# Tokens held in four phases instead of two around a depthwise convolution, on eight cores

## The chip, the cores and the metric

The kernel runs on all 8 cores of one Trainium2 chip. Each core computes half of one of the four sequences (2048 of 4096 tokens), with no exchange between cores. The metric is the device time in microseconds of the slowest core. Before the change the median of three runs is 989.3 us (989.25 to 990.63).

## The reference, cut to what matters

```python
h = concat([meta_tokens(16), x], axis=1)               # per sequence, T = 16 + 4096, 1024 channels
u = rms_norm(h, g_mix)
z = u @ w_in                                           # 1024 -> 5 * 1024
a = z[..., :1024] * sigmoid(z[..., 1024:2048])         # GLU
a = depthwise_conv(a, w_dw, width 31, centred) + b_dw  # 1024 channels
a = silu(layer_norm(a, ln_g, ln_b))                    # statistic over the 1024 channels of a token
y_conv = a @ w_conv_out
p = z[..., 2048:3072]
m = window_mean(p, 2 / 4 / 8 / 16 per 256 channels) - p
y_pool = (einsum(m, w_pool) * pool_scale) @ w_pool_out
gA, gB = sigmoid(z[..., 3072:] + b_gate)
h = h + (gA * y_conv + gB * y_pool) @ w_o
v = rms_norm(h, g_ffn)
h = h + (silu(v @ w_ffn_gate) * (v @ w_ffn_up)) @ w_ffn_down     # d_ff = 2816
out = rms_norm(h, g_final)[:, 16:]
```

## The kernel before, in words

Channels lie on the 128 partitions (8 chunks `c` of 128 channels), tokens along the free dimension. A core takes its 2048 tokens plus a halo, `EXT` = 2080 columns. The tokens are kept in two phases: `uT` is `[128, 8, 2, 1040]`, all even tokens of a chunk and then all odd ones.

A small recorder (`Sched`) takes every operation in the order in which the Python emits it, adds the semaphore waits that its reads and writes need, and replays the list of each engine. So each engine works strictly in emission order; `op` and `dma` (lines 164 and 172) are the helpers, and all records carry the line of a helper: L370 is every matmul but the convolution's (L664), L381 every ScalarE activation, L384, L391 and L397 VectorE or GpSimd operations, L199 a DMA issue. Eight PSUM banks exist: banks 6 and 7 hold statistics, and `nb()` hands out the other six in a ring, so a matmul tile waits until the tile six before it has been read out. Work that is not urgent (the pooling windows, the layer norm steps) sits in a list `bg`, and `pump(n)` emits the next n of its items on the spot.

The order is: the start (`START`, a list written out by hand: squares, RMS statistic, normalised `uT`, and the `pool` projections); then for each chunk `c` the stage of the convolution (lines 682 to 693): `vg(c)` computes value and gate in five pieces of 416 tokens into `aT`, GpSimd writes `aT` to a DRAM scratch `ad` in two DMAs (`a_out`), `conv(c-2)` runs, and then SyncE issues `im2col(c)`: 16 DMAs that read `ad` back into `rep`, each channel four times, shifted by one column each. `rep` has four buffers (two for each chunk; the last chunk has two of its own), so `im2col(c)` fills what `conv(c-2)` has just read.

The convolution (`conv`, line 653) is a matmul against a sparse weight: one rhs row is one of 16 channels, 2 phases and 4 shifts (16 x 8 = 128 rows), so one matmul covers 8 taps, and four of them (`q`) cover 31. The output has 32 columns (16 channels by 2 phases), and four such matmuls (`j`) fill the 128 PSUM partitions next to each other. A group `g` of 64 channels has two tiles of 512 columns, read out by two ScalarE operations each (`d` and its square `dsq`), and VectorE adds them up in `acc_s` and `acc_q`.

After the last `conv(7)`: four tiles of gate B, the layer norm statistic (`ln_stat`: a matmul with `pmask` sums over partitions of the same phase, for two halves of 512 columns), `fold(g)` (folds `w_pool` into `w_pool_out`, into `weff`), gate tiles, and among them the steps of `ln_steps` (subtract the mean on VectorE or GpSimd, multiply with 1/std, then `silu` on ScalarE and a DMA by SyncE which brings rows of 64 channels by 2 phases into rows of 128 channels, `cell`). `P` is the pool product with `weff`, `C` the convolution's output product, which needs the `cell` DMAs. The output projection and the feed-forward part follow.

The source of one read-back DMA and its destination are (lines 648 to 651):

```python
for j in range(4):
    for r in range(2):
        src = bass.AP(a_d, (128 * c + 64 * i + 16 * j) * EXT + HE * r, [[EXT, 16], [1, 4], [1, RW]])
        S.dma(SP, rep_sem[r_i], rep[r_i][r::2, j, 0:RW], src, val=tot)
```

Of the kernel before, what the change touches and what calls it, by code (L numbers as in the profile page):

```python
# [22 lines left out]
HALO = 15  # L23
# [3 lines left out]
HE = EXT // 2  # L27
HP = PW // 2
# [13 lines left out]
RW = TOK // 2 + 12  # L42
RWP = 1040
# [8 lines left out]
PC_BDW, PC_LNG, PC_LNB = 48, 64, 80  # L52
PC_COLS = 96
# [148 lines left out]
def build_nc():  # L202
# [18 lines left out]
    cw_d = din("cw", [NG, 128, 512])  # L221
# [3 lines left out]
    a_d = nc.dram_tensor("ad", [KC, 128, 2, HE], BF16, kind="Internal")  # L225
# [34 lines left out]
    oW = reserve(16384)  # L260
# [4 lines left out]
    uT = at("uT", [128, KC, 2, HE], BF16, oA)  # L265
# [3 lines left out]
    mT = at("mT", [128, KC, 2, TOK // 2], BF16, oM)  # L269
# [4 lines left out]
    def dof(g, h):  # L274
        return oB + (g // 2) * EXT * 4 + (2 * (g % 2) + h) * 2048

    d_sb = [at(f"d{g}", [128, 2 * TT], F32, dof(g, 0)) for g in range(NG)]
    cell = [at(f"cell{c}", [128, 2, 2, 2, TT], BF16, oB + c * EXT * 4) for c in range(KC)]
    actX = [[cell[g // 2][:, g % 2, h, 0, :] for h in range(2)] for g in range(NG)]
    actT = [[cell[c][:, b % 2, b // 2, 1, :] for b in range(NB)] for c in range(KC)]  # L280
    mrg = [[cell[c][:, b % 2, b // 2, 0, :] for b in range(NB)] for c in range(KC)]
    acc_s = at("acc_s", [128, TOK // 2], F32, oW)
    acc_q = at("acc_q", [128, TOK // 2], F32, oW + 4096)
    pmask = at("pmask_s", [128, 128], F32, oW + 8192)
    cw = [at(f"cw{i}", [128, 4, 4, 32], BF16, oW + 8704 + i * 1024) for i in range(3)]
    cw.append(alloc("cw3", [128, 4, 4, 32], BF16))
# [8 lines left out]
    rep = [at(f"rep{i}", [128, 4, RWP], BF16, o) for i, o in  # L295
           enumerate((z, z + 8 * RWP, oB + 6 * EXT * 4, oB + 7 * EXT * 4, z + 24064, z + 32384))]
    z += 2 * 4 * RWP * 2
    dsq = [at("dsq0", [128, 2 * TT], F32, z), at("dsq1", [128, 2 * TT], F32, oW + 11776)]
# [3 lines left out]
    aT = [at(f"aT{i}", [128, 2, HE], BF16, z + i * EXT * 2) for i in range(2)]  # L302
# [3 lines left out]
    z += 2 * S_W * 4  # L306
    assert z <= oZ + NZT * 2048, (z - oZ, NZT * 2048)
# [225 lines left out]
    def s1_norm(p, h):  # L533
        o, n = PIECES[p]
        for k in range(4 * h, 4 * h + 4):
            stt(DVE, uT[:, k, :, o // 2:(o + n) // 2], par(xb[p][:, k, :]), pcc(PC_GMIX, k), par(psum[7][:, 0:n]),
                ALU.mult, ALU.mult)

    def pool_tile(p, c):
        o, n = PIECES[p]  # L540
        b = nb()
        for k in range(KC):
            mm(par(b[:, 0:n]), w(f"pool{c}", k), uT[:, k, :, o // 2:(o + n) // 2], k == 0, k == KC - 1)
# [6 lines left out]
    def windows(c, ti):  # L550
# [8 lines left out]
        m = mT[:, c, :, t0 // 2:(t0 + n) // 2]  # L559
# [52 lines left out]
    def load_cw(g):  # L612
        S.dma(POOL, cw_sem[g % 4], cw[g % 4][:].rearrange("p j q m -> p (j q m)"), cw_d.ap()[g])
# [25 lines left out]
    def im2col(c):  # L639
# [5 lines left out]
        for i in range(2):  # L645
            r_i = rix(2 * c + i)
            tot = rep_sem[r_i].count + 16 * 8
            for j in range(4):
                for r in range(2):
                    src = bass.AP(a_d, (128 * c + 64 * i + 16 * j) * EXT + HE * r, [[EXT, 16], [1, 4], [1, RW]])  # L650
                    S.dma(SP, rep_sem[r_i], rep[r_i][r::2, j, 0:RW], src, val=tot)

    def conv(c):
        pump_until(win_done, c)
        for g in (2 * c, 2 * c + 1):
            for h in range(2):
# [17 lines left out]
            elif g > 1:  # L674
                tt(DVE, acc_s[:], acc_s[:], d_sb[g][:], ALU.add)
# [478 lines left out]
```

How the kernel before makes its waits and increments, by code:

```python
def replay(e, rec):  # L190
    for o in rec.ops:
        if o[0] == "wait":
            e.wait_ge(o[1], o[2])
        elif o[0] == "ins":
            r = o[1](e)
            if o[2]:
                r.then_inc(rec.sem, 1)
        else:
            e.dma_start(out=o[1], in_=o[2]).then_inc(o[3], 16)
```

## Time and profile before

| | before |
|---|---|
| median of 3 runs | 989.3 us (989.25 to 990.63) |
| the profiled execution, its own time | 991.0 us |
| span of its slowest core (core 0) | 989.5 us |
| spans of all cores | 985.5 to 989.5 us |
| TensorE busy / VectorE / ScalarE / GpSimd | 97% / 44% / 29% / 16% |
| TensorE clock granted, core 0 | 0.997 on average |
| DMA moved | 105.81 MB |

The span runs from the first to the last instruction of a core. A matmul of 512 columns is recorded with 379 ns, but these overlap: what counts is the distance from one to the next. The rows that the prediction uses stand in a section of their own below.

### The profile page before, as it was taken

The page shows a single profiled execution, that of the slowest core. Times are in us where ns is not written, and L with a number is a line of the kernel's source. Part 1 is how long each engine was busy: PE and PEld are TensorE (multiplying, and loading weights), DVE is VectorE, ACT ScalarE, POOL GpSimd, SP SyncE. Part 2 cuts the span into 40 slices and gives each one's busy share as a digit, 9 for nine tenths or more (in the row PEclk, how much of TensorE's full clock was granted, in tenths as well). Part 3 has the DMA queues.
Part 4 walks back from the last instruction along what each step waited for, and adds up shares of the span by engine and source line. Part 5 has one row for each costly group of instructions (what it writes and reads, how often), then busy time and mean ns, then how long its engine had stood idle before and what let it go on. Part 6 is the DMA issues. An engine that isn't in the chain of part 4 may idle for free.

```text
span 989.5 us, 14699 instructions; the slowest of 8 cores (985.5 to 989.5 us)
## 1 busy us (share of the span) xinstructions
PE 962.3 (97%) x5176; PEld 474.0 (48%) x5176; DVE 433.1 (44%) x632; ACT 291.7 (29%) x486; POOL 154.9 (16%) x216
## 2 busy tenths in 40 slices
PE   3999999999899999999999999999999999999996
PEld 2755555554344444444444444444444444444485
DVE  4776689653885323233476212211112211342454
ACT  3853143356952121110544111111111111121121
POOL 3002221124740000001771110110000000000000
PEclk9999999999999999999999999999999999999999
DMA  9705988775773111226965444553222005122222
GB/s 212 233 4 98 217 215 177 231 171 119 132 170 62 22 20 24 32 32 155 356 165 133 74 82 90 101 98 47 34 31 43 12 1 181 75 85 85 85 86 85
DMA packets 41158, 105.81 MB, mean 107 GB/s; under 512 B 5760, under 2 KB 14208, under 8 KB 38400
## 3 DMA queue, kind: packets, MB, share of 16 engines
q0 software_dynamic: 21472, 51.06, 28.7%
q1 hardware_dynamic: 19616, 53.82, 16.3%
q8 instruction: 43, 0.70, 0.3%
q14 instruction: 27, 0.22, 0.1%
HBM read 115.80 MB, written 21.04 MB: 138 GB/s over the span
## 4 chain that ended last, share of the span: by engine, by line
PE 95%; DMA 2%; DVE 1%; POOL 1%; issue 1%; ACT 0%; DVEq 0%; ACTq 0%; POOLq 0%
PE ps L370 92%; PE ps L664 3%; DMA xb<-xp 1%; DMA wslot<-w_pool_out 1%; DVE uT L397 0%; POOL d L384 0%; DVE h2b L397 0%; POOL wslot L199 0%; ACT sqx L381 0%; DVE sqx L384 0%; ACT ps L381 0%; ACT sq L381 0%; DVE h2b L384 0%; DVEq L1033 0%; DVEq L193 0%
## 5 line engine op out<-in xcount | busy, mean ns | idle before, releaser
L370 PE MATMUL ps<-vT,wslot 128*128 128x512 bf16 x1408 | 304.4, 379 | 0.0
L370 PE MATMUL ps<-uT,wslot 128*128 128x416 bf16 (+3 forms) x1536 | 292.3, 349 | 3.1 <-DVE uT L397 2.3
L370 PEld LDWEIGHTS ps<-uT,wslot 128*128 128x128 bf16 x1536 | 151.1, 99 | 140.8 <-issue 12.6
L370 PEld LDWEIGHTS ps<-vT,wslot 128*128 128x128 bf16 x1408 | 137.7, 98 | 167.1 <-issue 1.6
L384 DVE TENSOR_TENSOR fT<-ps,sgf 128x512 bf16<-128x512 f32 x88 | 60.7, 691 | 228.8 <-PE ps L370 228.8
L370 PE MATMUL ps<-fT,wfd 128*128 128x512 bf16 (+1 forms) x880 | 153.2, 336 | 0.0
L381 ACT ACTIVATE sgf<-ps 128x512 f32<-128x512 f32 x88 | 52.5, 597 | 241.5 <-PE ps L370 234.2
L370 PEld LDWEIGHTS ps<-fT,wfd 128*128 128x128 bf16 x880 | 86.1, 98 | 67.8 <-issue 1.7
L370 PE MATMUL ps<-cell,wslot 128*128 128x512 bf16 x512 | 114.8, 379 | 0.0
L397 DVE SCALAR_TENSOR_TENSOR zt<-zt,ps 128x512 f32<-128x512 f32 x64 | 43.9, 687 | 106.1 <-PE ps L370 106.0
L381 ACT ACTIVATE zt<-ps,hb 128x512 f32<-128x512 f32 x64 | 43.9, 691 | 138.1 <-PE ps L370 138.1
L370 PEld LDWEIGHTS ps<-cell,wslot 128*128 128x128 bf16 x512 | 50.1, 98 | 61.1 <-issue 1.1
L370 PE MATMUL ps<-mT,weff 128*128 128x512 bf16 x256 | 59.8, 381 | 0.0
L381 ACT ACTIVATE sq<-h2b 128x512 f32<-128x512 f32 (+1 forms) x35 | 19.1, 544 | 105.4 <-DVE h2b L384 105.4
L384 DVE TENSOR_TENSOR h2b<-ps,h2b 128x512 f32<-128x512 f32 (+1 forms) x40 | 23.2, 583 | 61.4 <-PE ps L370 51.2
L199 POOL DMA_DIRECT2D wslot<-w_in x40 | 22.7, 584 | 150.7 <-PE ps L370 149.8
L199 POOL DMA_DIRECT2D wslot<-w_ffn_up x22 | 11.8, 537 | 202.1 <-PE ps L370 202.1
L381 ACT ACTIVATE sg<-ps 128x416 f32<-128x416 f32 x40 | 20.9, 524 | 75.1 <-PE ps L370 63.0
L370 PEld LDWEIGHTS ps<-mT,weff 128*128 128x128 bf16 x256 | 25.3, 99 | 30.9 <-issue 1.1
L384 POOL TENSOR_TENSOR ac<-ac,sq 128x512 f32<-128x512 f32 x28 | 35.7, 1274 | 20.1 <-ACT sq L381 18.3
L384 DVE TENSOR_TENSOR aT<-ps,sg 128x416 bf16<-128x416 f32 x40 | 23.6, 589 | 33.8 <-PE ps L370 30.2
L384 DVE TENSOR_TENSOR ac<-ac,sq 128x512 f32<-128x512 f32 (+1 forms) x34 | 20.1, 590 | 28.3 <-ACT sq L381 28.3
(76 smaller groups left out, 610.6 us busy)
## 6 DMA issues: line engine op xcount, KB each, us to landing
rep<-ad SPq DMA_DIRECT2D x128, 129.5 KB, 4.7
wslot<-w_in POOLq DMA_DIRECT2D x40, 256.0 KB, 7.0
h1d<-h1b SPq DMA_DIRECT2D x4, 2048.0 KB, 10.1
h2b<-h1d SPq DMA_DIRECT2D x4, 2048.0 KB, 13.7
h1b<-xr SPq DMA_DIRECT2D x3, 2048.0 KB, 19.6
out<-h2b SPq DMA_DIRECT2D x3, 2048.0 KB, 8.1
wslot<-w_ffn_gate POOLq DMA_DIRECT2D x22, 256.0 KB, 5.3
wslot<-w_ffn_up POOLq DMA_DIRECT2D x22, 256.0 KB, 5.2
```

Of the source, the lines that this page charges most:

```text
L199: e.dma_start(out=o[1], in_=o[2]).then_inc(o[3], 16)
L370: S.op(PE, lambda e: e.matmul(out, lhsT=lhsT, rhs=rhs, start=start, stop=stop), [lhsT, rhs], [out], signal=stop if signal is None else signal)
L381: S.op(ACT, lambda e: e.activation(out=out, in_=in_, func=func, scale=scale, **kw), reads, [out])
L384: S.op(eng, lambda e: e.tensor_tensor(out=out, in0=a, in1=b, op=op), [a, b], [out])
L397: S.op(eng, lambda e: e.scalar_tensor_tensor(out=out, in0=a, scalar=s, in1=b, op0=op0, op1=op1), [a, b] + ([] if isinstance(s, float) else ...
L664: S.op(PE, lambda e, o=o, lt=lt, r_=r_, q=q, j=j: e.matmul(o, lhsT=lt, rhs=r_, start=(q == 0), stop=(q == 3), tile_position=(0, 32 * j)), ...
```

## The change

The number of phases goes from 2 to 4 (`PH`), in all layouts that hold tokens in the mixer part (`uT`, `aT`, `ad`, `mT`, `cell`, the host's `xp`, `xr` and `out`). A 16-column shift replaces the 15-column one (`HALO`). A convolution row is now 8 channels by 4 phases by 4 shifts, that is 16 token positions; 31 taps need three matmuls per tile instead of four. A tile is 32 channels (`i`) by 4 phases, with all 512 columns. The layer norm statistic covers 512 columns at once, after VectorE has added the two tiles (`i`) of `acc_s` and of `acc_q`. `silu` works on four blocks of 256 columns per chunk and half, each followed by its own DMA. Reads and writes of `psb` (float32, tokens in order) go through `alt` with a step of 4 elements instead of 2.

```diff
-HALO = 15
+HALO = 16
+PH = 4
...
-HE = EXT // 2
-HP = PW // 2
+HE = EXT // PH
+HP = PW // PH
...
-RW = TOK // 2 + 12
+RW = TT + 5
...
-    a_d = nc.dram_tensor("ad", [KC, 128, 2, HE], BF16, kind="Internal")
+    a_d = nc.dram_tensor("ad", [KC, 128, PH, HE], BF16, kind="Internal")
...
-    uT = at("uT", [128, KC, 2, HE], BF16, oA)
+    uT = at("uT", [128, KC, PH, HE], BF16, oA)
...
     def par(ap):
-        return ap.rearrange("p (e x) -> p e x", e=2)
+        return ap.rearrange("p (e x) -> p e x", e=PH)
 
     def alt(ap):
-        return ap.rearrange("p (x e) -> p e x", e=2)
+        return ap.rearrange("p (x e) -> p e x", e=PH)
+
+    def two(ap):
+        return ap.rearrange("p (f x) -> p f x", f=2)
...
-            for j in range(4):
-                for r in range(2):
-                    src = bass.AP(a_d, (128 * c + 64 * i + 16 * j) * EXT + HE * r, [[EXT, 16], [1, 4], [1, RW]])
-                    S.dma(SP, rep_sem[r_i], rep[r_i][r::2, j, 0:RW], src, val=tot)
+            for j in range(8):
+                src = bass.AP(a_d, (128 * c + 64 * i + 8 * j) * EXT, [[1, 4], [HE, 32], [1, RW]])
+                S.dma(SP, rep_sem[r_i], rep[r_i][:, j, 0:RW], src, val=tot)
...
-            for h in range(2):
+            for i in range(2):
                 ps = nb()
-                for q in range(4):
+                for q, x0 in enumerate((0, 4, 5)):
                     for j in range(4):
                         o = ps[32 * j:32 * j + 32, :]
-                        lt = cw[g % 4][:, j, q, :]
-                        x0 = h * TT + 4 * q
-                        r_ = rep[rix(g)][:, j, x0:x0 + TT]
+                        lt = cw[g % 4][:, i, q, j, :]
+                        r_ = rep[rix(g)][:, 4 * i + j, x0:x0 + TT]
...
-    def ln_stat(h):
-        tok = slice(h * TT, (h + 1) * TT)
-        pm, pq = (nb(), nb()) if h else (psum[6], psum[7])
-        mm(pm[:], pmask[:], acc_s[:, tok], True, True)
-        mm(pq[:], pmask[:], acc_q[:, tok], True, True)
...
+    def ln_stat():
+        pm, pq = psum[6], psum[7]
+        for acc, ps in ((acc_s, pm), (acc_q, pq)):
+            tt(DVE, acc[:, :, 0, :], acc[:, :, 0, :], acc[:, :, 1, :], ALU.add)
+            mm(two(ps[:]), pmask[:], acc[:, :, 0, :], True, True)
...
     def silu(h, c):
-        for g in (2 * c, 2 * c + 1):
-            act(actX[g][h], dpart(g, h), AF.Silu, bias=pc[:, PC_LNB + g:PC_LNB + g + 1],
-                scale=pc[:, PC_LNG + g:PC_LNG + g + 1])
-        for g in (2 * c, 2 * c + 1):
-            r0 = 64 * (g % 2)
-            S.dma(SP, rg_sem[h * KC + c], cell[c][r0:r0 + 64, :, h, 1, :], actX[g][h], val=32)
+        for q in range(4):
+            G = 4 * c + q
+            act(cell[c][:, h, q, 0, :], dcell[c][:, h, q, :], AF.Silu, bias=pcc(PC_LNB, G), scale=pcc(PC_LNG, G))
+        for q in range(4):
+            S.dma(SP, rg_sem[h * KC + c], cell[c][32 * q:32 * q + 32, h, :, 1, :], cell[c][:, h, q, 0, :], val=64)
...
-            if g == 0:
-                if h:
-                    cp(DVE, psum[6][:], mean)
-                    cp(DVE, psum[7][:], rstd)
-                    zfree.append(ids[1])
...
     for g in range(4):
         wps_scale(g)
     Bm(0, 0)
     Bm(0, 1)
     Bm(0, 2)
-    for h in range(2):
-        ln_stat(h)
+    ln_stat()
     Bm(0, 3)
     release("gB0")
-    for h in range(2):
-        ln_rstd(h)
+    ln_rstd()
     bg.extend(ln_steps(0))
     bg.extend(ln_steps(1))
```

## Rows read from the trace of the kernel before

**Rows 1.** The page: TensorE in all, and in 40 slices of the span.

```profile
PE 962.3 (97%) x5176; PEld 474.0 (48%) x5176; DVE 433.1 (44%) x632; ACT 291.7 (29%) x486; POOL 154.9 (16%) x216
PE   3999999999899999999999999999999999999996
```

**Rows 2.** TensorE's waits: what for, us in total, times, longest.

```profile
PE ps L370 <- DMA wslot<-w_pool_out: 2.5, 1, 2.5
```

**Rows 3.** Timeline of TensorE, 125 to 250 us: start, duration, form, count.

```profile
128.55 14.24 PE L370 MATMUL ps<-uT,wslot 128*128 128x416 bf16 x80
...
146.30 14.51 PE L370 MATMUL ps<-uT,wslot 128*128 128x416 bf16 x80
...
235.02 3.64 PE L664 MATMUL ps<-rep,cw 128*32 128x512 bf16 x64
238.59 5.37 PE L370 MATMUL ps<-uT,wslot 128*128 128x512 bf16 x24
243.80 1.02 PE L370 MATMUL ps<-acc_s,pmask_s 128*128 128x512 f32 x2
...
247.23 1.89 PE L370 MATMUL ps<-uT,wslot 128*128 128x512 bf16 x8
```

**Rows 4.** The read-back's DMA issues on SyncE: ns, first and last start.

```profile
L199 SPq DMA_DIRECT2D rep<-ad x128: 514/594/1903, 101.2 to 229.7; - x128
```

**Rows 5.** The same DMAs, 214 to 240 us: issue to landing, minimum, median, maximum.

```profile
DMA to landing us min/median/max: 3.9/5.6/6.7
```

**Rows 6.** DMA queues from 101 to 235 us: packets, MB, share of 16 engines.

```profile
q1 hardware_dynamic: 10240, 16.98, 42.5%
q0 software_dynamic: 5616, 10.28, 40.7%
```

**Rows 7.** DMA rate from 143 to 161 us, in 40 slices.

```profile
GB/s 169 114 246 92 134 194 252 120 4 9 36 105 100 168 105 114 159 159 153 123 157 233 211 154 106 113 308 382 364 382 355 336 318 318 327 318 308 290 249 32
```

**Rows 8.** Timeline of VectorE: in brackets its idle time before, and who ended it.

```profile
145.83 1.23 DVE L384 TENSOR_TENSOR acc_s<-acc_s,d 128x1024 f32<-128x1024 f32 x1 [1.14 <-ACT d L381]
...
155.70 0.58 DVE L384 TENSOR_TENSOR aT<-ps,sg 128x416 bf16<-128x416 f32 x1
...
173.51 0.59 DVE L384 TENSOR_TENSOR aT<-ps,sg 128x416 bf16<-128x416 f32 x1
...
238.25 1.33 DVE L384 TENSOR_TENSOR acc_s<-acc_s,d 128x1024 f32<-128x1024 f32 x1 [11.72 <-ACT d L381]
```

**Rows 9.** Groups by form: count, busy us, mean ns; idle before, releaser.

```profile
L381 ACT ACTIVATE cell<-d,pc_s 128x512 bf16<-128x512 f32 x32 | 24.3, 814 | 6.0 <-DVE d L384 6.0
L381 ACT ACTIVATE sq<-h2b 128x512 f32<-128x512 f32 x21 | 13.2, 630 | 78.3 <-DVE h2b L384 78.3
L381 ACT ACTIVATE sq<-h2b 128x256 f32<-128x256 f32 x14 | 5.8, 417 | 27.1 <-DVE h2b L384 27.1
L397 DVE SCALAR_TENSOR_TENSOR mT<-s,psb 128x1024 bf16<-128x1024 f32 x12 | 14.7, 1223 | 0.4
L384 DVE TENSOR_TENSOR s<-s 128x1024 f32<-128x1024 f32 x12 | 14.6, 1220 | 0.5
```

**Rows 10.** Timeline of ScalarE, GpSimd and TensorE around the folds.

```profile
252.57 0.71 ACT L381 ACTIVATE acc_q<-acc_q,eps_s 128x512 f32<-128x512 f32 x1
...
267.54 1.09 ACT L381 ACTIVATE weff<-ps 128x512 bf16<-128x512 f32 x2
...
252.98 6.20 POOL L384 TENSOR_TENSOR d<-d,zt 128x512 f32<-128x512 f32 x5
259.13 0.59 POOL L199 DMA_DIRECT2D wslot<-w_pool_out  x1
...
265.50 2.93 PE L370 MATMUL ps<-wslot,wslot 128*128 128x512 bf16 x7 [2.49 <-DMA wslot<-w_pool_out]
268.22 14.45 PE L370 MATMUL ps<-mT,weff 128*128 128x512 bf16 x64
```

**Rows 11.** One stretch: busy us of PE, PEld, DVE, ACT, POOL; clock; DMA share; GB/s.

```profile
259.00:268.00 9.00, 6.33 (x25) 2.58 (x24) 8.69 (x15) 9.00 (x15) 7.67 (x11) 0.88 0.81 153
```

More of the change, by code:

```diff
@@ L259, in build_nc @@
     oM = reserve(KC * TOK * 2)
-    oW = reserve(16384)
+    oW = reserve(16896)
     oS = reserve(NSLOT * 2048)
@@ L294, in build_nc @@
     z = oZ
[L295 to L298, printed above, removed]
+    RB = 16 * HE
+    rep = [at(f"rep{i}", [128, 8, HE], BF16, o) for i, o in
+           enumerate((z, z + RB, oB + 6 * EXT * 4, oB + 7 * EXT * 4, z + 24064, z + 32384))]
+    z += 2 * RB
+    dsq = [at("dsq0", [128, 2, 2, 256], F32, z), at("dsq1", [128, 2, 2, 256], F32, oW + 8192)]
     z += 4096
@@ L301, in build_nc @@
     z += 2 * PW * 4
-    aT = [at(f"aT{i}", [128, 2, HE], BF16, z + i * EXT * 2) for i in range(2)]
+    aT = [at(f"aT{i}", [128, PH, HE], BF16, z + i * EXT * 2) for i in range(2)]
     z += 2 * EXT * 2
@@ L733, in C @@
         stt(DVE, zt[i][:], zt[i][:], 1.0, ps[:], ALU.add, ALU.mult)
-        tt(DVE, mrg[c][b], zt[i][:], zt[j][:], ALU.add)
+        tt(DVE, mrg[c][b], two(zt[i][:]), two(zt[j][:]), ALU.add)
         zfree.append(i)
@@ L786, in send @@
         def send(n):
+            mean = half2(zt[ln_ids[1]], h)
             while sent[0] < min(n, len(far)):
@@ L944, in build_nc @@
             for k in range(KC):
-                mm(ps[:], w(f"wo{c}", k), mrg[k][b], k == 0, k == KC - 1)
+                mm(two(ps[:]), w(f"wo{c}", k), mrg[k][b], k == 0, k == KC - 1)
             h = h1b[b][:, c, :]
@@ L1078, in _host_inputs @@
     for col, v in ((PC_BDW, arr("b_dw")), (PC_LNG, arr("ln_g")), (PC_LNB, arr("ln_b"))):
-        pc[:, col:col + NG] = np.repeat(v.reshape(NG, 64), 2, 1).T
-    zero = np.zeros((1, D), f32)
-    wdw = arr("w_dw")
-    taps = np.stack([np.concatenate([wdw, zero], 0), np.concatenate([zero, wdw], 0)], 0)
-    vals = taps.reshape(2, 4, 8, NG, 4, 16).transpose(3, 5, 2, 4, 1, 0)
-    cw = np.zeros((NG, 16, 8, 4, 4, 16, 2), f32)
-    for i in range(16):
-        cw[:, i, :, :, :, i, :] = vals[:, i]
+        pc[:, col:col + 2 * NG] = np.repeat(v.reshape(2 * NG, 32), PH, 1).T
+    wdw = arr("w_dw").reshape(KW, NG, 2, 4, 8)
+    cw = np.zeros((NG, 4, 8, PH, 2, 3, 4, 8, PH), f32)
+    for q in range(3):
+        for a in range(4):
+            if q == 2 and a < 3:
+                continue
+            for pi in range(PH):
+                for po in range(PH):
+                    tap = PH * (4 * q + a if q < 2 else 8) + pi - 1 - po
+                    if 0 <= tap < KW:
+                        for ch in range(8):
+                            cw[:, a, ch, pi, :, q, :, ch, po] = wdw[tap, :, :, :, ch]
     pmask = np.zeros((128, 128), f32)
-    pmask[0::2, 0::2] = 1.0 / D
-    pmask[1::2, 1::2] = 1.0 / D
+    for e in range(PH):
+        pmask[e::PH, e::PH] = 1.0 / D
     T = SEQ + NMETA
@@ L1135, in _gather @@
 def _gather(results, core):
-    o = np.asarray(results[core]["out"]).reshape(2, 2, 128, KC, TT)
-    return o.transpose(0, 4, 1, 3, 2).reshape(TOK, D)
+    o = np.asarray(results[core]["out"]).reshape(2, 2, 128, KC, 2, 256)
+    return o.transpose(0, 5, 1, 4, 3, 2).reshape(TOK, D)
 _NC_CACHE = {}
```

116 lines of the change are left out of this document (60 added, 56 removed).

## The prediction

> **What bounds the kernel now.** I read the page first: TensorE is busy for 962.3 of 989.5 us, and outside the first slice it has almost no hole [rows 1]. So the time is TensorE's work plus what it waits for; a change is worth what it takes from TensorE's row, unless something beside TensorE is nearly late already. For the slowest core, the waits name one pause in the middle, 2.5 us for a load of `w_pool_out` [rows 2]. Then I looked at what runs beside TensorE in the stages that the change touches, and found four things near their limit.
>
> First, the read-back into `rep`. Its 128 DMAs are issued from 101.2 to 229.7 us [rows 4], and the last ones take 3.9 to 6.7 us to land [rows 5], so `rep` for group 15 is complete near 234.4. TensorE needs it halfway through conv(7), at 235.02 + 1.78 = 236.8 [rows 3]: 2.4 us of slack. From 101 to 235 the hardware queue carries 16.98 MB in 42.5% of sixteen engines, the software queue (weights, `ad`, `cw`) 40.7% [rows 6]; together 83%.
>
> Second, VectorE. It idles 1.14 us before 145.83 and not again before the next two rows, and frees the first value bank of vg(4) at 155.70 + 0.58 = 156.3 and that of vg(5) at 174.1 [rows 8]. TensorE wants the first for its fourth pair, 7 tiles of 1.42 us after 146.30, at 156.2. That is why vg(4) takes 14.51 us [rows 3], where vg(2), the same eighty matmuls, takes 14.24.
>
> Third, VectorE after conv(7): its last two pairs of additions start at 238.25 and run back to back, four of about 1.23 us, to 243.2 [rows 8], and the statistic's matmuls begin at 243.80 [rows 3]. Fourth, ScalarE and GpSimd around the folds: the slot for the late `w_pool_out` load is asked for only when GpSimd has done five subtractions, and ScalarE is busy for all 9.00 us from 259 to 268 [rows 10, 11].
>
> **The change part by part.**
>
> *Fewer convolution matmuls.* conv(7) goes from 235.02 to 238.59 [rows 3], 3.57 us for 16 groups of four matmuls side by side, 0.223 us each. Twelve groups take 2.68, so 0.89 is saved, 7.1 us over eight chunks.
>
> *One statistic.* The fp32 matmuls take 247.23 - 243.80 = 3.43 us [rows 3]; half goes, -1.7. But the sum needs another VectorE addition first (0.65 us). Today VectorE is done 8.2 us after conv(7) starts [rows 3, 8]; with tiles that come a little sooner and the addition it is about 8.6. TensorE is there after 2.68 + 5.2 = 7.9, and waits 0.7. Net -1.0. Behind it stands only gate tile Bm(0,3), which is merely shifted.
>
> *Smaller silu.* A 512-column activation of this group is busy for 24.3/32 = 0.76 us; 256 columns less save 630 - 417 = 0.21 [rows 9], so four of 0.55 replace two of 0.76: +0.7 us of ScalarE per chunk and half. Five chunks lie ahead of the last `weff` copy (+3.4), and one Ln and Exp go (-1.3, the span from 252.57 to the next copy). ScalarE reaches the copy at 267.54; P(0,0) wants its result at its seventh matmul, 268.22 + 1.3 = 269.5 [rows 10]. The copy would end near 270.1: +0.6. The bounds are 0 (the load hides it) and +2.1. Their DMAs double in number at half the size; SyncE issues one in about 0.6 us [rows 4], 19 us a half beside about 20 us of `silu`, hidden.
>
> *More blocks in a moving operand* (four for two, two for one). Cut in two, 416 columns take (14.24 - 0.07)/80 = 177 ns, 0.426 a column; uncut, 512 take (243.80 - 238.59)/24 = 217 ns, 0.424 [rows 3]. I take nothing; at 1 ns a cut the 2300 matmuls concerned would cost 2 us.
>
> *Steps of four elements.* `psb` is written and read at 16 bytes apart instead of 8. At 8 bytes it costs nothing: 1223 ns against 1220 for the form without steps [rows 9]. No row shows 16. Bounds: nothing, or double the 1.07 us in which 1024 elements stream. I take nothing, since the nearest row shows nothing; the other end is a rival. The Trainium skill (SBUF — State Buffer, Door 1: The DMA port swizzle) says lines are 16 bytes and full bandwidth wants two hits in each, and then that fp32 may step by 4 for free; by the first half this edit costs, by the second it doesn't. No row decides.
>
> *The read-back.* The count (16 a chunk) and the bytes stay (64 rows of 2072 bytes become 128 of 1034). But the order of the source changes. Before, the outermost extent of the source pattern is 16 channels and the destination has 64 partitions; now the source begins with `[1, 4]`, four shifts, against 128 partitions. If the hardware queue deals a DMA out over the engines by the outermost extent, it finds 16 shares before and 4 now, and all read-back goes through the same four of sixteen engines. Nothing in the trace has such a form, so the price is bounded: nothing if it is dealt out by rows, and otherwise this. The fastest slice with mainly read-back shows 382 GB/s [rows 7]; a quarter is 95.5 GB/s, and 16.98 MB take 178 us. The four engines also carry their share of the software queue, 40.7% of 134 us = 54.5 us in today's crowd [rows 6], perhaps half of it when twelve engines idle: I take 41. 178 + 41 = 219 us. The low end is 178 + 27 = 205; the high end takes today's shares whole: 0.425 x 134 x 4 + 54.5 = 282. I take four engines as the likelier: sixteen divides the outermost extents that this queue's read-back has today (16 and 64), so its even spread is just what dealing by the outermost extent gives, and it would give four now. The Trainium skill (DMA: Bandwidth & Descriptors, Why a DMA increments its semaphore by 16 and not by 1) states the rule: the engine count is the largest number up to 16 that divides the slowest dimension of both sides, 16 before and 4 after. No row here shows a transfer with fewer than 16 shares, so the trace neither confirms nor contradicts it.
>
> **The sum.** The stage becomes bound by the queue. im2col(c) can be issued as soon as im2col(c-1) is through, since TensorE's 16.9 us per chunk are less than 219/8 = 27. The read-back begins at 101.2, so group 15 lands at 320.2 instead of being used at 236.8: +83.4 us. The savings of conv(0) to conv(6), and all of VectorE's tightness, vanish in waits of about 10 us before each convolution. What follows counts fully: half of conv(7) -0.45, statistic -1.0, ScalarE +0.6, and after a pause TensorE starts at half clock: in 259 to 268 it waited 2.5 us and was granted 0.88 [rows 10, 11], 1.1 us lost; after 10 us of pause I take 1.7. Together +0.8. Span 989.5 + 84.2 = 1073.7; the profiled execution's 991.0 becomes 1075.2, and the median, 1.7 below it, 1073.5 us. With the stage's ends: 1059 to 1137.
>
> **The rivals.**
>
> *All engines still share the read-back: faster.* For it: every read-back today spreads well (382 GB/s [rows 7]), bytes and DMA count are the same. Against it: the extent of four. The time: conv -7.1. VectorE gives part back: its dense run starts only 1.1 us sooner (0.89, and 0.25 for the smaller tile), while TensorE comes 1.8 us sooner to vg(4) and 2.7 to vg(5), so about 1.5 us is waited [rows 3, 8]. Statistic -1.0, ScalarE +0.6. TensorE reaches group 15 by 2.2 us sooner relative to the last `ad` write, against 2.4 us of slack [rows 3 to 5]: +0.3. Sum -5.8: 983.5 us. It decides from the first conv: if `rep` lands within some 17 us per chunk, this case holds.
>
> *The step of 16 bytes costs double, with all engines: no change.* VectorE has 1.07 us more for each of eight `mT` operations before 181 us, in a stage where it has no slack: backlog +1.6 at vg(4), +3.7 at vg(5) against today, where TensorE would be 1.8 and 2.7 earlier. That eats 6.4 of 7.1 us. ScalarE's writes of `psb` grow by what they stream, 0.21 us per 256 columns [rows 9]; for those in the crowded start I put 1.5, between nothing and 5 (24 of them). -0.7 - 1.0 + 0.6 + 0.3 + 1.5 = +0.7: 990 us. For it: a step never shown; against it: 8 bytes cost 3 ns in 1220 [rows 9].
>
> **How the numbers follow.** Four engines 0.68, all engines and faster 0.20, the step 0.12. The likeliest gives 1073.5, its own range is 1045 to 1137. The range over the cases runs from 981 to 1125, since the other two hold three in ten. A measurement here tells about 0.2% from no change. Faster: 0.20 + 0.03; same: 0.05; slower: the rest, 0.72.
>
> **What would show it.** Four engines: in the rows of `rep` the time from issue to landing well over 6 us and the last issue near 310 us; TensorE waiting for a DMA into `rep` before each conv, about 10 us; the mean DMA share from 101 to 320 near a quarter plus the weights; TensorE's clock below 1.00 behind the pauses. After conv(7) a tail of about 752 us. The matmuls: 384 on `rep`, 2.68 us a chunk if not waiting. The step: `mT` operations at 1223 ns or above 2000, the writes of `psb` about the same or markedly longer. The forecast is wrong if the last `rep` DMA is issued before 240, and its size if the stage lasts less than 205 or more than 282 us.

## The result, and the profile after

The changed kernel takes 1130.0 us (median of 1120.7, 1130.0 and 1130.1) against 989.9 for the kernel before in the same session: ratio 1.1385, 95% interval 1.134 to 1.143. It is slower by 140 us. A fourth run took 1151.1 us: in some runs of every kernel one die is slower at a lower clock whatever the kernel, and all medians and ratios from here on are without those runs. I had forecast slower, 1073.5 us, with 1125 as the upper end; the median lies 5 us beyond it, and one of the three runs inside.

The slowest core (core 5) has a span of 1128.1 us. First the page: TensorE in all and by 40 slices, and the chain that ended last. They answer to [rows 1].

```profile
PE 999.3 (89%) x5044; PEld 477.2 (42%) x5044; DVE 445.5 (39%) x631; ACT 316.1 (28%) x514; POOL 155.7 (14%) x216
...
PE   4788947566718999999999999999999999999997
...
PEclk9988978888757788999999999999999999999999
...
PE 75%; SPq 13%; DMA 4%; DVE 3%; issue 2%; ACT 2%; POOL 0%; DVEq 0%; ACTq 0%; POOLq 0%
```

The row `PEclk` is the granted clock in tenths. TensorE has 132 fewer matmuls on record and is busy longer, because its clock is lower (0.928 on average for 0.997). Its holes lie in slices 1 to 12, and SyncE's queue (SPq), which only issues DMAs, is 13% of the chain. The waits of TensorE say on what (compare [rows 2]):

```profile
PE ps L677 <- DMA rep<-ad: 81.7, 9, 15.4
PE ps L376 <- DVE sqx L390: 13.6, 3, 12.7
PE ps L376 <- DVE uT L403: 12.8, 14, 3.4
PE ps L677 <- DVE acc_s L390: 6.5, 1, 6.5
...
PE ps L376 <- DMA wslot<-w_pool_out: 1.1, 1, 1.1
```

The wait for the read-back is the forecast one. The one for `uT` is not: it was 2.3 us before. The read-back's issues (to hold against [rows 4]), and the queues while it runs (against [rows 6]):

```profile
L199 SPq DMA_DIRECT2D rep<-ad x128: 511/1384/7177, 126.7 to 354.0; - x128
```

```profile
q0 software_dynamic: 5854, 11.56, 26.2%
q1 hardware_dynamic: 16896, 16.94, 21.4%
```

The first issue comes at 126.7 instead of 101.2, the last at 354.0 instead of 229.7, and the median issue takes 1384 ns for 594. In the 236 us of the second view the read-back uses 21.4% of sixteen engines; if four engines carry it, that is 0.214 x 236.3 x 4 = 202 us for each. With an even share of the software queue (0.262 x 236.3 = 62) it would be 264 us, 12% more than the stage has, so that queue's work isn't spread evenly or packet times overlap; these shares alone don't show that the four are full. The run e2 below shows it.

TensorE's timeline in that stage (compare [rows 3]): the second group of each convolution waits, and its 24 matmuls then take 2.75 us, where 24 unpaused ones take 1.49 (in 229.5 to 232.1 us the granted clock is 0.50).

```profile
212.57 1.49 PE L677 MATMUL ps<-rep,cw 128*32 128x512 bf16 x24
229.42 2.75 PE L677 MATMUL ps<-rep,cw 128*32 128x512 bf16 x24 [15.36 <-DMA rep<-ad]
232.10 14.57 PE L376 MATMUL ps<-uT,wslot 128*128 128x416 bf16 x80
...
363.49 2.75 PE L677 MATMUL ps<-rep,cw 128*32 128x512 bf16 x24 [3.00 <-DMA rep<-ad]
```

VectorE's timeline shows what I had not forecast (compare [rows 8]): it waits for TensorE before it writes `uT`, and for the scratch DMA before the fourth piece of `aT`.

```profile
84.02 4.82 DVE L403 SCALAR_TENSOR_TENSOR uT<-xb,pc_s,ps 128x448 bf16<-128x448 f32 x8 [11.47 <-PE ps L376]
...
139.77 0.59 DVE L390 TENSOR_TENSOR aT<-ps,sg 128x416 bf16<-128x416 f32 x1 [8.24 <-DMA ad<-aT]
```

Two stretches of the kernel after, and then the first of them in the kernel before (columns as in [rows 11]):

```profile
52.00:90.00 38.00, 31.13 (x140) 15.17 (x140) 18.64 (x26) 19.09 (x25) 0.00 (x0) 0.81 0.00 0
...
366.20:437.90 71.70, 69.51 (x259) 28.34 (x256) 48.05 (x74) 50.23 (x94) 34.37 (x36) 0.80 0.54 108
```

```profile
52.00:90.00 38.00, 38.00 (x205) 20.15 (x204) 28.52 (x35) 17.06 (x29) 4.25 (x8) 1.00 0.36 58
```

So the 138.6 us between the spans of the two slowest cores fall into three parts, each from start and end times of the timelines: the start, up to the first read-back, 126.7 - 101.2 = +25.5; the stage, from there to the end of conv(7), 239.5 for 137.4 = +102.1; and all after it, 761.9 for 750.9 = +11.0.

The third part isn't the change's. It stands in cores 4 and 5 alone: behind conv(7) they take 762 us each, the other six cores 750 to 751, and the cores of the kernel before 749 to 751. The stretch from above in core 3 and in core 4:

```profile
366.20:437.90 71.70, 67.98 (x302) 29.73 (x301) 50.97 (x80) 50.82 (x94) 30.85 (x34) 0.98 0.57 118
```

```profile
366.20:437.90 71.70, 69.47 (x258) 28.32 (x259) 49.38 (x77) 49.62 (x92) 32.79 (x35) 0.81 0.55 111
```

The first two parts stand in all cores: the read-back begins at 125.3 to 129.2 us (98.3 to 101.2 before), and the stage lasts 237 to 245 us (137.4 to 137.9 before).

The costs by form (compare [rows 9]). `mT` took 1223 ns before; the three `psb` forms took 584, 406 and 564.

```profile
L403 DVE SCALAR_TENSOR_TENSOR mT<-s,psb 128x1024 bf16<-128x1024 f32 x12 | 24.0, 1996 | 0.4
L390 DVE TENSOR_TENSOR aT<-ps,sg 128x416 bf16<-128x416 f32 x40 | 23.6, 589 | 65.4 <-DMA ad<-aT 38.1 <-PE ps L376 14.4 <-ACT sg L387 6.9
```

```profile
L387 ACT ACTIVATE cell<-d,pc_s 128x256 bf16<-128x256 f32 x64 | 33.1, 599 | 2.0 <-DVE d L390 2.0
...
L387 ACT ACTIVATE psb<-ps 128x448 f32<-128x448 f32 x16 | 15.7, 983 | 14.7 <-PE ps L376 14.7
L387 ACT ACTIVATE psb<-ps 128x256 f32<-128x256 f32 x24 | 15.1, 630 | 9.8 <-PE ps L376 9.3 <-DVE sqx L390 0.5
...
L387 ACT ACTIVATE psb<-ps 128x416 f32<-128x416 f32 x8 | 7.4, 920 | 9.2 <-PE ps L376 9.2
```

### The profile page after: what moved, and what is told of

It reads as the page before. It is cut to its first block, busy times and chain, and to the rows that moved or that the text cites. A ratio compares the mean times of both kernels' runs of the same rounds, so it can differ in the third digit from the quotient of the medians.

```text
span 1128.1 us, 14541 instructions; the slowest of 8 cores (1113.6 to 1128.1 us)
## 1 busy us (share of the span) xinstructions
PE 999.3 (89%) x5044; PEld 477.2 (42%) x5044; DVE 445.5 (39%) x631; ACT 316.1 (28%) x514; POOL 155.7 (14%) x216
## 4 chain that ended last, share of the span: by engine, by line
PE 75%; SPq 13%; DMA 4%; DVE 3%; issue 2%; ACT 2%; POOL 0%; DVEq 0%; ACTq 0%; POOLq 0%
PE ps L376 74%; SPq L199 13%; DMA rep<-ad 3%; DVE uT L403 1%; DMA ad<-aT 1%; ACT cell L387 1%; DMA xb<-xp 1%; DVE sqx L390 1%; PE ps L677 1%; ACT ps L387 0%; DVE mT L403 0%; ACT psb L387 0%; DVE h2b L403 0%; ACT sqx L387 0%; ACT weff L387 0%
## 5 line engine op out<-in xcount | busy, mean ns | idle before, releaser
L376 PE MATMUL ps<-uT,wslot 128*128 128x416 bf16 (+3 forms) x1536 | 316.5, 363 | 17.0 <-DVE uT L403 12.8
L376 PEld LDWEIGHTS ps<-uT,wslot 128*128 128x128 bf16 x1536 | 154.6, 101 | 178.0 <-issue 72.9
L376 PE MATMUL ps<-cell,wslot 128*128 128x512 bf16 x512 | 117.4, 385 | 0.0
L677 PE MATMUL ps<-rep,cw 128*32 128x512 bf16 x384 | 36.1, 531 | 88.2 <-DMA rep<-ad 81.7
L376 PE MATMUL ps<-mT,weff 128*128 128x512 bf16 x256 | 64.1, 400 | 1.1 <-ACT weff L387 1.0
L677 PEld LDWEIGHTS ps<-rep,cw 128*32 128x32 bf16 x384 | 12.0, 118 | 108.6 <-issue 105.3
L387 ACT ACTIVATE d<-ps,pc_s 128x512 f32<-128x512 f32 x32 | 22.1, 690 | 96.8 <-PE ps L677 96.6
L387 ACT ACTIVATE psb<-ps 128x256 f32<-128x256 f32 (+2 forms) x48 | 38.2, 796 | 33.8 <-PE ps L376 33.3
L390 DVE TENSOR_TENSOR acc_s<-acc_s,d 128x1024 f32<-128x1024 f32 x14 | 17.1, 1224 | 72.9 <-ACT d L387 72.7
## 6 DMA issues: line engine op xcount, KB each, us to landing
rep<-ad SPq DMA_DIRECT2D x128, 129.2 KB
h1d<-h1b SPq DMA_DIRECT2D x4, 2048.0 KB, 10.3
```

The source lines that it names most:

```text
L376: S.op(PE, lambda e: e.matmul(out, lhsT=lhsT, rhs=rhs, start=start, stop=stop), [lhsT, rhs], [out], signal=stop if signal is None else signal)
L387: S.op(ACT, lambda e: e.activation(out=out, in_=in_, func=func, scale=scale, **kw), reads, [out])
L390: S.op(eng, lambda e: e.tensor_tensor(out=out, in0=a, in1=b, op=op), [a, b], [out])
L677: S.op(PE, lambda e, o=o, lt=lt, r_=r_, q=q, j=j: e.matmul(o, lhsT=lt, rhs=r_, start=(q == 0), stop=(q == 2), tile_position=(0, 32 * j)), ...
```

## The experiments

Ratios are to the kernel before, run beside each (990.6 to 991.1 us). "A", "B", "L" and "S" in the expectations are the theories each names.

**The order of the source alone.** The changed kernel with channels outermost, and the kernel before with shifts outermost (weight rows permuted to match in both):

```diff
-                src = bass.AP(a_d, ..., [[1, 4], [HE, 32], [1, RW]])          # after
+                src = bass.AP(a_d, ..., [[HE, 32], [1, 4], [1, RW]])          # e1
-                    src = bass.AP(a_d, ..., [[EXT, 16], [1, 4], [1, RW]])     # before
+                    src = bass.AP(a_d, ..., [[1, 4], [EXT, 16], [1, RW]])     # e2
```

> The changed kernel with one edit: the source of the read-back begins with 32 rows instead of 4 shifts ([[HE, 32], [1, 4], [1, RW]]), and the convolution weights' rows are put in the same order. DMA count, bytes and the 1034-byte pieces stay. Theory (outermost extent of 4 confines the read-back to four engines): the time from issue to landing of a rep DMA falls back to 3 to 9 us, the waits of 82 us for rep go, the clock stays at 1.00 in the convolution stage. The start (126.7 us instead of 101.2 before the first read-back) doesn't change, since it lies ahead of it, so about 989 + 25 - 5 = 1005 to 1015 us. Rival (short or unaligned pieces are slow on any number of engines): stays above 1100 us.

> The kernel before with the one property added: the source of the read-back begins with the 4 shifts ([[1, 4], [EXT, 16], [1, RW]]), weight rows reordered to match; two phases, 2072-byte pieces, everything else as before. Theory (four engines): the stage becomes bound by the queue, 128 DMAs of 16 pieces per engine at 85 to 109 ns give 174 to 222 us plus the software queue's share of 55 to 80, against 134 us today: 1080 to 1150 us. Rival (it is the four phases, not the order): stays at 989 us.

e2 measured 1073.5 us, ratio 1.083 [1.082, 1.085]. Its waits and its issues:

```profile
PE ps L664 <- DMA rep<-ad: 65.6, 7, 13.7
```

```profile
L199 SPq DMA_DIRECT2D rep<-ad x128: 507/1214/3768, 101.1 to 305.5; - x128
```

The order alone, with two phases, costs 82.8 us, and its stage is 220.7 us from the first issue to the end of conv(7), against 137.4: +83.3. This is the forecast mechanism at the forecast size. In the last part of its stage, where little but the read-back runs, the sixteen engines are busy for about a quarter, and the rate (last column, GB/s) is about a quarter of the 382 of [rows 7]:

```profile
284.00:296.00 12.00, 3.90 (x36) 1.41 (x40) 2.36 (x2) 2.54 (x4) 0.00 (x0) 0.64 0.26 99
```

e1 measured 1052.2 us, ratio 1.061 [1.058, 1.063]. The read-back now lands in 5.1 us, its issue takes 603 ns in the median, and no wait for `rep` is left among TensorE's large ones; still the kernel is 61 us slower than before and 37 above the end of what I expected, with its first read-back at 130.4. So a second cause exists:

```profile
PE ps L677 <- DVE aT L390: 19.7, 6, 4.5
...
PE ps L376 <- DVE uT L403: 12.5, 13, 3.4
PE ps L376 <- DVE aT L390: 9.0, 3, 7.1
```

**Is the second cause the step of 16 bytes?** e3 puts such steps into the kernel before, e4 takes them out of e1. In both the pooling branch gets its tokens in another order and computes something else.

```diff
+        return ap.rearrange("p (x e f) -> p e f x", e=2, f=2)     # e3: psb written and read in steps of 4
-        return ap.rearrange("p (x e) -> p e x", e=PH)             # e1
+        return ap.rearrange("p (e x) -> p e x", e=PH)             # e4: no step
```

> The kernel before, but psb is written by ScalarE and read by VectorE for mT with a step of 4 float32 (16 bytes) instead of 2, in the same number of elements and operations. The tokens of the pooling branch end up in another order, so that branch computes something else. Theory (the 16-byte step is what makes psb 796 instead of 470 ns and mT 1996 instead of 1223 ns): those two groups show the longer durations, the first read-back is issued 15 to 25 us later than at 101.2, time 1003 to 1015 us. Rival (the late start comes from the four-block uT and PSUM patterns or something else of the change): 989 to 991 us.

> The changed kernel with the read-back order of e1 and, besides, psb written and read without a step (the rows of psb are kept in phase order as blocks, so the pooling windows add up the wrong tokens: that branch computes something else). All else of the change is in. Theory (four engines and the 16-byte step are all that costs): the sum of the fast case holds, 7.1 us of convolution, 1.0 of statistic saved, 1.5 waited for VectorE, less than 1 at the folds: 982 to 986 us, faster than before by 0.4 to 0.7%. Rival (the change has further costs, such as more blocks per operand, twice the silu DMAs, or ScalarE at the folds): 989 us or more.

e3: 994.5 us, ratio 1.0037 [1.0023, 1.0050]. e4: 1056.4 us, 1.0625 [1.0574, 1.0676], no better than e1. The step costs 3.8 us by itself and is not the second cause. In e4 VectorE stands idle 59.2 us for the DMA that reads `aT`.

**The recorder's granule.** VectorE writes one piece of `aT` while a DMA reads another; they share no byte. But the recorder tracks reads and writes in granules of `GRAN` = 32 bytes. With two phases a row of `uT` is 2080 bytes and a piece of `aT` 416 bytes, both multiples of 32. With four they are 1040 and 208, odd multiples of 16, so that neighbours share a granule, and the recorder adds a wait. With `GRAN = 16` the instructions stay as they are and only such waits go; `s_pe`, `s_act` and `s_dve` are semaphores of engines, those with `d_` of DMAs. For instance:

```text
-L403 SCALAR_TENSOR_TENSOR uT<-xb_101,pc_s,ps 128x4x64 [waits s_act,d_x1,s_pe]
+L403 SCALAR_TENSOR_TENSOR uT<-xb_101,pc_s,ps 128x4x64 [waits s_act,d_x1]
-L390 TENSOR_TENSOR aT_116<-ps,sg_115 128x4x104 [waits s_pe,s_act,s_dve,d_ad0]
+L390 TENSOR_TENSOR aT_116<-ps,sg_115 128x4x104 [waits s_pe,s_act]
```

e5 is the changed kernel with that one line, e6 has the order as well, e7 also lacks the step (pooling as in e4), and e8 gives the kernel before a granule of 64 bytes, in which its own pieces (13 x 32 bytes) share.

```diff
-GRAN = 32
+GRAN = 16        # e5, e6, e7;   GRAN = 64 in e8
```

> The changed kernel with one edit: the recorder tracks reads and writes in granules of 16 bytes instead of 32 (GRAN). In the changed layouts a phase row of uT is 1040 bytes and a piece of aT 208 bytes, odd multiples of 16, so neighbouring pieces share a 32-byte granule, and the recorder adds waits between operations that touch no common byte. Not an instruction changes, only waits. The read-back still begins with the 4 shifts. Theory B (e1 stands 62 us above before because of these waits): the first read-back is issued near 101 us, the aT operations no longer wait for the ad DMA, and the time falls from 1130 to what the four engines alone cost, as in e2: 1065 to 1085 us. Rival (the waits are harmless, e1's excess comes from other parts of the change): 1125 us or more.

> The changed kernel with both edits: granules of 16 bytes and the read-back's source beginning with the 32 rows. It computes the reference. Theory B: what is left of the costs is the 16-byte step (3.8 us in e3 at most), so 982 to 990 us, and the fast case's sum less the step would be 987. Rival (something else of the change costs): above 995 us.

> As e6, and psb without a step, as in e4 (the pooling branch computes something else). Theory: the fast case of the sum, 982 to 986 us, 2 to 5 us below e6. Rival (the step costs nothing here since VectorE has room once the convolution's rhythm is set by TensorE): within 1 us of e6.

> The kernel before with one edit: granules of 64 bytes instead of 32. Its phase row of uT is 2080 bytes and its piece of aT 416 bytes, odd multiples of 32, so the same neighbours share a granule as in the changed kernel at 32. Same instructions, only waits are added. Theory B: the same waits appear (VectorE's uT for TensorE, aT for the ad DMA), the start takes 20 to 30 us longer and the convolution stage 30 to 40: 1030 to 1060 us. Rival: within 5 us of 989.

e8: 1031.4 us, ratio 1.041 [1.040, 1.043], as expected. The kernel before, its layout untouched, gets the same waits and starts its read-back at 126.0 instead of 101.2:

```profile
PE ps L370 <- DVE uT L397: 10.8, 12, 3.4
PE ps L664 <- DVE aT L384: 10.0, 4, 4.3
PE ps L370 <- DVE aT L384: 3.2, 2, 2.2
```

e5: 1101.4 us, 1.111 [1.110, 1.113], above the 1065 to 1085 expected; e6: 1010.8 us (1012.8 over all its runs, the figure in the expectations that follow), 1.0205 [1.019, 1.022], above 982 to 990; e7: 1009.0 us, 1.018 [1.017, 1.020], above 982 to 986. Together with e1 this is a square:

| | shifts outermost | channels outermost |
|---|---|---|
| granule 32 | 1130.0 (after) | 1052.2 (e1) |
| granule 16 | 1101.4 (e5) | 1010.8 (e6) |

The order costs 78 to 91 us, the granule 29 to 41. In the 1130.0 stand some 10 us of the tail of two cores; against the run at 1120.7 the granule costs 19 and the order 69 in that row and column. The granule costs less beside the four engines, since there its part in the stage is hidden under the queue and only its start counts: e5 begins its read-back at 103.3, 23.4 us sooner than the changed kernel, while its stage lasts no less (245.4 us). In e5 TensorE's large waits in the stage are all for `rep` (99.7 us, 10 times).

**The row length on four engines.** e5 and e2 both have the shifts outermost and no added waits, yet e5 is 28 us slower, nearly all of it in the stage: 242 to 245 us by core, 216 to 221 in e2. Their read-back queues, e2 from 101.1 to 312 us, then e5 from 103.3 to 343:

```profile
q1 hardware_dynamic: 8488, 16.56, 21.1%
```

```profile
q1 hardware_dynamic: 16832, 16.88, 21.3%
```

If four engines carry them, e2 has 0.211 x 210.9 x 4 = 178 us of it on each and e5 0.213 x 239.7 x 4 = 204. A row of 2072 bytes takes 84 ns of an engine (share x 16 x window / packets), one of 1034 takes 49, 1.16 times as much per byte. That is as large as the difference of the stages. But no run changes the row length alone on four engines, and e5 also has 12% more in the software queue (11.5 for 10.3 MB).

**What is left: 1010.8 against the 983.5 of my case in which all engines share.** The queues from 101 to 245 us, first e6, then the kernel before with its rows of 2072 bytes cut in two (g1, 101 to 240 us; [rows 6] is the uncut one):

```profile
DMA  9999999999999899998899987997989998999984
...
q1 hardware_dynamic: 18432, 16.95, 50.4%
q0 software_dynamic: 5580, 11.06, 42.9%
```

```profile
DMA  8999889889999899983499962998549788499992
...
q1 hardware_dynamic: 18432, 16.98, 44.5%
q0 software_dynamic: 5616, 10.28, 39.6%
```

In e6 (core 1, its slowest) the engines are busy 93% of the stage, with hardly a gap to catch up in. The runs g1, g2, g4 and g5 add this load to the kernel before, or take it from e6.

```diff
-                for r in range(2):                                   # before
+                for x in (0, RW // 2):                               # g1: 128 rows of 1036 bytes a DMA
+                    src = bass.AP(a_d, ... + x, [[HE, 32], [1, 4], [1, RW // 2]])
...                                                                   # g2: g1, scratch writes cut in two,
+    cw_d = din("cw", [NG, 128, 768])                                 #     192 KB of weights a group
                                                                      #     (some buffers move to make room)
-            if g + 4 < NG:                                           # e6
-                load_cw(g + 4)                                       # g4: only the first four loads
+                n = 16 if j >= 4 and 2 <= c < KC - 1 else 32         # g5: a quarter fewer rows, c = 2 to 6
```

> The kernel before, in two phases, with each read-back row of 2072 bytes brought as two of 1036 by two DMAs; 16 DMAs a chunk as before, outermost extent 32, so all sixteen engines; the weight rows are reordered to match. Same bytes, twice the rows, that is the shape of the changed kernel's read-back and nothing else of it. Theory A (what is left between 1012.8 and the 984 of the fast case is the DMA stage, full because 1034-byte rows take more engine time per byte): the hardware queue's share from 101 us to the last read-back rises from 42.5% to about 52% and the sum with the software queue to over 90%; TensorE has 0.9 us more a chunk here than in the changed kernel, so part of it stays hidden: 994 to 1006 us. Rival B (short rows cost nothing; the rest is the order of the work or the layer norm part): 988 to 992 us, share of the hardware queue within 2 points of 42.5%.

> As the run with the short read-back rows, and also the two other things that the change does to the queues: the writes into the scratch cut in two (rows of 624 and 416 bytes for 1248 and 832) and 192 KB of convolution weights a group for 128 KB (the third part of 512 columns is loaded and not used). A: the software queue's share rises by 3 to 5 points, the scratch writes land in about 7 us in place of 4.6, and the time is 4 to 12 us above the run with the short read-back rows alone: 998 to 1015. B: within 3 us of the kernel before.

> The changed kernel with the engine order and the 16-byte granule mended (1012.8 us), and of the 16 loads of convolution weights only the first four; later groups use old weights, so the convolution computes something else. TensorE's work is the same. That leaves out 12 loads of 192 KB, some 2.4 of the 28 MB of the stage, on the software queue. A: the queue is what TensorE waits for (17.4 us for rep in one core), so the waits fall by about 10 us and the time is 995 to 1005. B: 1009 or more, since the read-back itself is unchanged.

> The same mended kernel (1012.8 us); in chunks 2 to 6 four of each eight read-back DMAs bring 64 rows for 128, a quarter of the rows of these chunks and so 16% of all read-back rows; TensorE reads old data there, so the convolution computes something else. DMA count and TensorE's work are the same. A: the hardware queue's part of the stage falls by 16% (some 11 us of engine time in 144), the waits for rep nearly vanish, 988 to 1000 us. B: within 3 us of 1012.8. If it reaches 984 to 988, the fast case of the forecast (983.5, and 3.8 for the 16-byte step) was right but for the queue's load.

g1: 991.4 us, 1.0009 [0.9998, 1.0020]: short rows alone cost nothing that can be told, though the row of 1036 bytes takes some 54 ns of engine time and the row of 2072 some 92 (share x 16 engines x 90 us / rows, from 130 to 220 us). A fell here: the kernel before has room for it. g2: 995.8 us, 1.0063 [1.0036, 1.0090], short of the 998 to 1015 of A. g4: 1007.4 us, 1.0173 [1.0142, 1.0204], whose interval overlaps that of e6 (1.019 to 1.022); g5: 1006.4 us, 1.0137 [1.0097, 1.0177]. g5 takes some of the loss, g4 may, and neither takes it all.

Three more on the weight loads. h1 moves two of the first four loads behind the second read-back; h2 makes two loads in all (the convolution computes something else); h3 is h1 without the 16-byte step (pooling as in e4).

```diff
-    for g in range(4):
+    for g in range(2):
         load_cw(g)
     vg(1)
     im2col(1)
+    for g in range(2, 4):
+        load_cw(g)
```

> The mended kernel (1012.8 us) with the loads of convolution weights for groups 2 and 3 issued after the second read-back (some 115 us) instead of at 100 us; same work. Theory A (the early wait is the burst of loads competing with the first read-back): rep for chunk 0 is complete by 125, the early waits of 3 to 10 us vanish and with them VectorE's 3.8 us for aT in part; the late wait stays: 1000 to 1009. Rival B (the early wait is the read-back's own length at 1034 bytes a row): within 3 us of 1012.8.

> The mended kernel with only the first two loads of convolution weights, every later group using these (the convolution computes something else; TensorE's work and the read-back are the same). A: neither place has a load beside the read-back, no core waits more than 3 us for rep, and the time is 988 to 996. B: 1005 or more, near the 1009.1 of the run with the first four loads.

> The mended kernel without the step of four in the pooling buffer (phases blockwise, so the pooling branch computes something else; 1009.0 us) and with the later loads of the run before last. 996 to 1006 us by A, and within 3 us of 1009.0 by B. Its least disturbed core shows the floor: 983 to 985 us if the fast case of the forecast was complete but for the queue, 987 to 989 if VectorE's wait for aT and the later weff are terms that it priced too low.

h1: 1012.8 us, 1.019 [1.012, 1.026], no gain that can be told, and its slowest core still waits 4.8 us for `rep` at conv(0); the burst at 100 us is not the cause of the early wait. h2: 1004.4 us, 1.015 [1.011, 1.019], not told apart from g4 and short of the 988 to 996 expected. h3: 1010.3 us, 1.018 [1.017, 1.020]; its least disturbed core ends at 986.6, its slowest at 1009.6. The waits of these two, core 7 and core 5:

```profile
PE ps L677 <- DVE acc_s L390: 3.0, 1, 3.0
...
PE ps L677 <- DMA rep<-ad: 0.8, 1, 0.8
...
PE ps L376 <- DVE aT L390: 0.5, 1, 0.5
```

```profile
PE ps L677 <- DMA rep<-ad: 19.9, 4, 12.1
```

The same program on the same chip thus loses between 1 and 20 us to the read-back, by core.

The last three ask whether rows that are no multiple of 4 bytes cost more, or the sum of the load decides. k1 is e6 with 1032 bytes for 1034, k2 is g1 with 1038 and 1034 for 1036, k3 takes both loads away, as h2 and g5 do (the convolution computes something else in k1 and k3).

```diff
-RW = TT + 5                      # e6
+RW = TT + 4                      # k1, third matmul from column 4
+                for x, n in ((0, 519), (519, 517)):      # k2
```

> The mended kernel (1012.8 us) with read-back rows of 1032 bytes for 1034; the third matmul of a tile reads from column 4 instead of 5, so the convolution computes something else, with the same work. Theory L (rows that are no multiple of 4 bytes cost more): the row falls from 55 to 66 ns to 52 to 55, and the time to 995 to 1003 us. Theory S (the sum of the load, whatever the length): 56 ns or more, and within 3 us of 1012.8.

> The kernel before with halved read-back rows, as in the first of these runs (991.7 us), but cut 519 + 517 elements, 1038 and 1034 bytes, both no multiple of 4. L: 56 to 60 ns a row and 993 to 1000 us. S: 52 to 55 ns as with 1036 bytes and 990 to 993 us.

> The mended kernel with only two loads of convolution weights (1004.4 us alone) and a quarter fewer read-back rows in chunks 2 to 6 (1006.4 us alone); the convolution computes something else, TensorE's work is the same. S: the two add, 996 to 999 us, and what waits for rep is left stands at conv(0) alone; the rest over 983.5 is VectorE's wait for aT (3.8), weff (2.3) and w_pool_out (2). L: about 1003 or more, since the rows keep their length.

k1: 1010.8 us, 1.020 [1.017, 1.023]. k2: 991.1 us, 1.0003 [0.9993, 1.0014]. The length is not it, on either kernel. k3: 998.6 us, 1.007 [1.005, 1.009], as the sum of load has it: h2 takes 6.4 us from e6, g5 4.4, together 10.8, and k3 takes 12.2 (each figure within some 2 to 4 us). In e6 the slowest core's longest wait stands at the second group of conv(6); in k3 that one is gone, and what its slowest core still loses to `rep` stands at conv(0) alone, again with half clock behind it (0.50 from 136.0 to 138.6 us). First e6, then k3:

```profile
238.67 2.75 PE L677 MATMUL ps<-rep,cw 128*32 128x512 bf16 x24 [12.38 <-DMA rep<-ad]
```

```profile
125.96 1.49 PE L678 MATMUL ps<-rep,cw 128*32 128x512 bf16 x24
135.96 2.75 PE L678 MATMUL ps<-rep,cw 128*32 128x512 bf16 x24 [8.51 <-DMA rep<-ad]
```

No variant of the changed kernel that computes the reference beats the kernel before; the best, e6 and h1, are 2% slower.

## Why the prediction was right and wrong

*Four engines: the mechanism was right.* Its place and its sign hold, and where it stands alone, in e2, its size too: +82.8 us. By the Trainium skill (DMA: Bandwidth & Descriptors, Why a DMA increments its semaphore by 16 and not by 1) the engine count is the largest number up to 16 that divides the slowest dimension of both sides; e1 and e2 agree with it (0.26 of sixteen engines busy at 99 GB/s in e2).

*The step that failed: "The read-back begins at 101.2".* It began at 126.7. I took the start of the kernel over unchanged, since the edits there seemed to alter layouts and not work. I had read of the recorder that it adds the waits which reads and writes need, and did not ask in what unit it compares them. The layout with 1040 and 208 bytes makes it add waits between pieces that share no byte. e8 shows this alone on the kernel before (+40.6 us), e5 and e6 show it by its removal. In the changed kernel it is +25.5 us in the start. Neither the forecast nor a rival had it, and the range ended below the result: e5, in which only this is mended, takes 1101.4 us, inside it.

*Second, a mis-sized term: "178 us" for the read-back's bytes on four engines.* I divided bytes by a quarter of the best rate, which rows of 2072 bytes had reached, and so took rows of half the length at the same price per byte. e2, with the long rows, has just 178 us; the changed kernel has 202 and e5 204. From the first issue to the end of conv(7) I had 220 us (219 and half of conv(7)); measured are 239.5, within the ends of 205 and 282 that I gave the stage. That the row length is what costs the 19 us is argued from the queues' rows, since the larger weight loads came with it.

*Third: the tail, +0.8 forecast, +11.0 measured in the slowest core, nothing in six others.* From 366.2 to 437.9 us TensorE is granted 0.80 in core 5 and 0.81 in core 4, although it is busy for 69.5 of 71.7 us; that is between its two levels (1.2 and 2.4 GHz). In cores 0 to 3 it is granted 0.96 to 0.98 after the same pauses for `rep`, and in e5, after ten of them, 0.96 to 1.00 in every core. So neither the pauses nor the change explain the 0.80, and no run shows what does. My 752 us for the tail stands against 750 to 751 where the clock is not low. The three misses, 25.5, 19 and 10 us, make up the 54.4 us between my span of 1073.7 and 1128.1. In the run at 1120.7 us, which is inside my range, no core's mean clock is below 0.942 (core 5 here: 0.928). By this sum the time would be inside in every one of the three runs without the start's 25.5 us.

*Right terms.* Convolution: 48 matmuls take 2.79 - 0.07 = 2.72 us (h2, k3), forecast 2.68. Blocks in the moving operand: 80 matmuls of four blocks take 14.24 us, as those of two did. Statistic: half of the fp32 matmuls and a wait of 0.8 us for `acc_s` (e6), forecast 0.7. `silu`: 599 ns a piece, forecast 550. VectorE's wait: 1.5 us in h3 (0.76 + 0.75), forecast 1.5. The saving of the change, though, never shows in the time.

*Wrong small terms.* The step of 16 bytes is not free: `mT` 1223 to 1996 ns, `psb` 406 to 630, 564 to 920, 584 to 983. As the rival had it, the step costs, 1.55 to 1.7 times, not double; in all it costs 3.8 us (e3), for the 6.4 + 1.5 that I had worked out. e6 against e7 gives 1.8, and their intervals overlap. By the Trainium skill (SBUF — State Buffer, Door 1: The DMA port swizzle) fp32 may step by 4 for free; the measurement decides against that half of the section. The folds: waits for `weff` and `w_pool_out` sum to 2.8 us before and 4.9 in e6, so +2.1 for the +0.6 forecast.

*The all-engines case was too fast.* I gave `rep` +0.3 there. With order and granule mended the kernel takes 1010.8, not 983.5. I had compared slack at one place, the last chunk; but the whole stage was at 83% of its engines [rows 6], the change adds rows, weights and shorter scratch writes to it, 93% in e6, and takes away the 0.9 us a chunk in which the queue could catch up. The longest wait of e6's slowest core, 12.4 us, is at conv(6), where I had not looked. k3 shows that the load carries about 12 of the 27.3 us, and the step carries 2 to 4. The rest, some 12 us, is not settled. In k3 it is in good part the wait at conv(0) in the slowest core (8.5 us), and which core that is differs by run; the row of 1034 bytes takes 55 to 66 ns by core in e6 and 52 to 56 in g1, where all else of the read-back is the same, and neither length (k1, k2) nor the first weight loads (h1) explain it.

## What to carry to other kernels

Before a layout changes, compute what its rows and pieces are modulo every unit that something in the program counts in: here a tracker of 32 bytes turned 208-byte pieces into waits worth 40 us, with no byte shared. Look at the outermost extent of a DMA's source: 4 for 16 alone was worth 83 us with bytes and count unchanged. Where a queue is nearly full through a stage, as here with 83%, price an edit by rows as well as bytes, by the sum over the stage and for the slowest core, not by the slack of one transfer. And before you explain a stretch of the slowest core, read the same stretch in the other seven: the tail of 11 us here belonged to two cores.

## What the runs showed of the hardware that I had not expected

Halving the length of a read-back row costs engine time, 54 ns for 1036 bytes against 92 for 2072, that is 1.17 times per byte, and no time of the kernel as long as the stage has gaps (g1). The DMA load of a full stage does not fall evenly: in h3 one core waits 0.8 us for `rep` and another 19.9. After a pause of 5 to 15 us for `rep` the next 24 matmuls take 2.75 us for 1.49, at a granted clock of 0.50, so each such pause costs 1.3 us beyond itself; after shorter ones it varies: 1.48 us behind 2.12 and 3.83 us of pause (h3, k1), 1.71 behind 4.30 and 2.75 behind 2.72 (e6, cores 4 and 0). And in one run of one program cores 4 and 5 were granted 0.80 through 72 us of steady work while cores 0 to 3 had 0.96 to 0.98.
